# Six of eight query tiles projected in the slots of the stick-breaking attention

## The chip, the cores and the metric

The kernel runs on one core of one Trainium2 chip. The metric is device time in microseconds of one execution. Before the change three runs took 2627.49, 2628.47 and 2636.64 us; the median is 2628.47.

## The reference

Two blocks run one after the other on a sequence of 512 tokens with 1024 features. The first holds two layers of chunked attention with relative bias beside retention. The second holds four feed-forward layers (width 2816), a convolution layer and one layer of stick-breaking attention with 16 heads of 64 features. The change touches that attention and the projections at its two sides:

```python
q = split_heads(u @ attn_w_q[i])
# stick_breaking_attention, per block of 128 queries, keys up to the block's end
z = jnp.einsum('bhqd,bhkd->bhqk', qb, kb) * scale
causal = s_pos < t_pos
log_beta = jax.nn.log_sigmoid(z)
log_one_minus = jnp.where(causal, jax.nn.log_sigmoid(-z), 0.0)
log_remain = lax.cumsum(log_one_minus, axis=3, reverse=True) - log_one_minus
weights = jnp.where(causal, jnp.exp(log_beta + log_remain), 0.0)
outs.append(jnp.einsum('bhqk,bhkd->bhqd', weights, vb))
# then
h = h + o @ attn_w_o[i]
```

## The kernel before, in words

All five engines run programs written out by hand; the order of the work on each is the order of the code, and semaphores tie them together. Features lie on partitions, tokens along the free axis. SyncE issues the DMAs of the weights, ScalarE rounds (names ending in `_hi`), GpSimd or VectorE subtracts to get the low part (`_lo`), TensorE multiplies, VectorE empties PSUM.

**A product of full precision** is three matmuls: high by high, low by high, high by low (`product`, lines 1372 to 1374, moving 128x512). Weights come in chunks of 1 MB into `raw`, two slots in turn. The queries' weights `w_q` are four chunks of two output tiles (128 features, one pair of heads); a tile is 8 products. `w_o` is four chunks of the same form. In `layer("q")` all eight tiles are projected, chunk by chunk, into PSUM banks 0 to 3; VectorE scales each tile with the row's inverse root mean square into `sb_q` (line 924). Keys and values were spilled to DRAM before the third feed-forward layer and are read back while the first query chunk runs (lines 468 and 469).

**The stick-breaking attention** handles a pair of heads at a time and, within a pair, four key tiles of 128 keys, from the last to the first, against 128, 256, 384 and 512 queries. That gives 32 slots of two units (one a head). For unit u:

- TensorE, `sb_scores` (L1710 and the mask, L1714): three products of the split keys and queries, into one of six PSUM banks.
- VectorE, `sb_absolute` (L1320): the absolute value into `tmp`. ScalarE, `sb_decay` (L840, exponential) and `sb_logs` (L845, logarithm).
- VectorE, `sb_softplus` (L1326) and `sb_rounds` (L1336, `soft_hi`); GpSimd, `soft_low` (L567, `soft_lo`).
- TensorE, `sb_arguments` (L1724): cumulative sums by triangular matrices, added onto the scores in the same bank.
- ScalarE, `sb_weights` (L835): the exponential into `stick`.
- TensorE, `sb_sums` (L1735): values times weights, into bank 4 or 5 by the pair's parity. After a pair VectorE rounds and splits the output (L1355, L1356).

On TensorE slot i holds `sb_scores(i)`, `sb_arguments` of slot i-2 and `sb_sums` of slot i-3. `sb_scores(i)` waits until the weights of slot i-3 are made, since the banks are used again. VectorE's iteration i takes softplus and rounding of the first unit of slot i-1, the two absolute values of slot i, softplus and rounding of the second unit of slot i-1, and where i is 6, 10, 14 and so on the output of a pair. ScalarE's iteration i takes two decays of slot i, then weights (slot i-2) and logarithms (slot i) in turn. GpSimd also stages the split queries and keys of the next pair (`stage_sb`, L558 and L561) between its `soft_low` calls. `soft_hi` and `soft_lo` lie over `x_hi` and `x_lo`.

After slot 31 GpSimd makes the low parts of `w_o`, and `out_layer("o")` runs.

## Time and profile before

| | us |
|---|---|
| median of three runs | 2628.47 |
| profiled execution | 2627.77 |
| its span, first to last instruction | 2626.0 |
| TensorE busy in the span | 2528.4 (96%) |
| ScalarE / VectorE / GpSimd busy | 710.4 / 1060.3 / 1007.6 |
| mean granted TensorE clock | 0.984 of full |

A profile row has the start, the duration, the engine, the line of the kernel, the operation, and what it writes and reads. What stands in brackets is the idle time of that engine ahead of the row and the operation that ended it. PEld is TensorE's weight load, which runs beside matmuls. The queries' projection runs from 2012 to 2058 us, the attention from 2059.6 to 2200.3 us, the output projection from 2201.6 us on. A granted clock of 1.00 is 2.4 GHz, 0.50 is 1.2 GHz; a number between is a mean over a stretch.

### The profile page before, as it was taken

Reading aid. Unit: us, or ns where it says so; the run is one execution under the profiler, and the core shown is the slowest. Engines: PE = TensorE matmul, PEld = TensorE weight load, DVE = VectorE, ACT = ScalarE, POOL = GpSimd, SP = SyncE. Lnnn points to the kernel's source line nnn. Section 1 sums busy time; section 2 is a strip of 40 time slices with the busy share of each in tenths; the row PEclk is TensorE's granted clock in tenths of the full one; section 3 lists DMA queues with packets and bytes.
Section 4 is the critical chain, followed back from the end, with each engine's and each line's share of the span. In section 5 each row is a group of like instructions: output and inputs, shape, how many; then the busy total and the mean of one; then the engine's idle time right before and its main releaser. Section 6 shows DMA issues by size and latency. Waiting matters only on the chain.

```text
span 2626.0 us, 30302 instructions
## 1 busy us (share of the span) xinstructions
PE 2528.4 (96%) x11686; PEld 1999.7 (76%) x11686; DVE 1060.3 (40%) x1579; ACT 710.4 (27%) x912; POOL 1007.6 (38%) x327
## 2 busy tenths in 40 slices
...
DMA packets 42033, 235.83 MB, mean 90 GB/s; under 512 B 5344, under 2 KB 5344, under 8 KB 21472
## 3 DMA queue, kind: packets, MB, share of 16 engines
...
q8 instruction: 57, 0.93, 0.2%
...
## 4 chain that ended last, share of the span: by engine, by line
PE 89%; DVE 6%; issue 3%; ACT 2%; POOL 0%; SPq 0%; DMA 0%; DVEq 0%; ACTq 0%; POOLq 0%
PE ps L1372 27%; PE ps L1374 26%; PE ps L1373 26%; PE ps L1724 2%; PE ps L1646 1%; PE ps L1735 1%; PE ps L1608 1%; PE ps L1579 1%; PE ps L1615 1%; PE ps L1710 1%; PE ps L1558 1%; PE ps L1386 1%; PE ps L1567 1%; DVE small L1089 1%; DVE score L1083 0%
## 5 line engine op out<-in xcount | busy, mean ns | idle before, releaser
L489 POOL TENSOR_TENSOR w_lo<-raw,w_hi 128x2048 fp32r<-128x2048 f32 (+1 forms) x212 | 901.6, 4253 | 1430.5 <-ACT w_hi L598 1430.5
L1372 PE MATMUL ps<-x_hi,w_hi 128*128 128x512 f32 x2048 | 809.3, 395 | 20.6 <-DVE x_lo L875 18.1
L1374 PE MATMUL ps<-x_hi,w_lo 128*128 128x512 f32 x2048 | 800.1, 391 | 0.0
L1373 PE MATMUL ps<-x_lo,w_hi 128*128 128x512 f32 x2048 | 799.4, 390 | 0.0
L598 ACT ACTIVATE w_hi<-raw 128x2048 fp32r<-128x2048 f32 (+1 forms) x220 | 385.3, 1751 | 350.8 <-PE ps L1374 343.4
L1372 PEld LDWEIGHTS ps<-x_hi,w_hi 128*128 128x128 f32 x2048 | 385.8, 188 | 112.3 <-issue 29.3
L1374 PEld LDWEIGHTS ps<-x_hi,w_lo 128*128 128x128 f32 x2048 | 385.8, 188 | 81.5
L1373 PEld LDWEIGHTS ps<-x_lo,w_hi 128*128 128x128 f32 x2048 | 386.3, 189 | 77.4
L985 DVE TENSOR_TENSOR tmp<-ps,rms_b 128x512 f32<-128x512 f32 x88 | 60.9, 692 | 589.2 <-PE ps L1374 578.6
L1372 PE MATMUL ps<-hid_hi,w_hi 128*128 128x512 f32 x704 | 278.1, 395 | 0.0
L1374 PE MATMUL ps<-hid_hi,w_lo 128*128 128x512 f32 x704 | 278.1, 395 | 0.0
L1373 PE MATMUL ps<-hid_lo,w_hi 128*128 128x512 f32 x704 | 278.1, 395 | 0.0
L687 ACT ACTIVATE tmp<-tmp 128x512 f32<-128x512 f32 x88 | 55.8, 634 | 699.1 <-DVE tmp L985 699.0
L1010 DVE SCALAR_TENSOR_TENSOR x<-ps,x 128x512 f32 x32 | 22.1, 692 | 389.2 <-PE ps L1374 389.2
L1374 PEld LDWEIGHTS ps<-hid_hi,w_lo 128*128 128x128 f32 x704 | 132.0, 187 | 32.4
L1372 PEld LDWEIGHTS ps<-hid_hi,w_hi 128*128 128x128 f32 x704 | 132.0, 187 | 32.3
L1373 PEld LDWEIGHTS ps<-hid_lo,w_hi 128*128 128x128 f32 x704 | 132.0, 187 | 32.2
L660 ACT ACTIVATE tmp<-x 128x512 f32<-128x512 f32 (+1 forms) x64 | 39.8, 633 | 337.7 <-DVE x L1010 236.8
L883 DVE TENSOR_TENSOR sq_sum<-sq_sum,tmp 128x512 f32<-128x512 f32 x80 | 116.2, 1453 | 9.8 <-ACT tmp L660 7.3
L993 DVE TENSOR_TENSOR hid_lo<-tmp,hid_hi 128x512 f32 (+1 forms) x88 | 84.9, 964 | 10.6
L567 POOL TENSOR_TENSOR soft_lo<-tmp,soft_hi 128x128 fp32r<-128x128 f32 (+3 forms) x64 | 55.4, 866 | 69.5 <-DVE soft_hi L1336 69.5
L1372 PE MATMUL ps<-w_hi,x_hi 128*128 128x512 f32 x192 | 77.9, 406 | 2.8 <-issue 2.8
...
## 6 DMA issues: line engine op xcount, KB each, us to landing
...
```

The costliest lines, as they stand in the source:

```text
L489: nc.gpsimd.tensor_tensor(w_lo[:, s, 0:w], raw[:, s, 0:w], w_hi[:, s, 0:w].bitcast(f32), ALU.subtract).then_inc(lo_ready, 1)
L567: nc.gpsimd.tensor_tensor(soft_lo[:, soft_span(u)], tmp[:, u % 6, 0:SPAN[u % 8 // 2]], soft_hi[:, soft_span(u)].bitcast(f32), ALU.subtract ...
L598: nc.scalar.activation(w_hi[:, s, 0:w], raw[:, s, 0:w], ACT.Copy).then_inc(hi_ready, 1)
L660: nc.scalar.activation(tmp[:, slot, :], x[:, j, :], ACT.Square).then_inc(squares_ready, 1)
L687: nc.scalar.activation(tmp[:, s, :], tmp[:, s, :], func, bias=bias_col).then_inc(gate_out, 1)
L883: nc.vector.tensor_tensor(sq_sum[:, :], sq_sum[:, :], tmp[:, slot, :], ALU.add)\
L985: nc.vector.tensor_tensor(tmp[:, s, :], ps[:, 2 * s, :], rms_b[:, :], ALU.mult)\
L993: nc.vector.tensor_tensor(hid_lo[:, j, :], tmp[:, 2 + s, :], hid_hi[:, j, :].bitcast(f32), ALU.subtract).then_inc(hidden_ready, 1)
L1372: nc.tensor.matmul(out, hi, src_hi, start=start, stop=False, skip_group_check=True)
L1373: nc.tensor.matmul(out, hi, src_lo, start=False, stop=False, skip_group_check=True)
L1374: return nc.tensor.matmul(out, lo, src_hi, start=False, stop=stop, skip_group_check=True)
L1724: ins = nc.tensor.matmul(ps[:, Z_BANK[u % 6], P * (r - later):SPAN[r]], weights[:, :], part[:, at], start=False, stop=later == r and part ...
```

## The change

Only the first query chunk (tiles 0 and 1) and the first tile of the second stay ahead of the attention. The other 40 products are issued two a slot ahead of the scores in slots 0 to 19, all into bank 5. VectorE scales tile t = 3 to 7 in slot 4(t-3)+3 behind that slot's absolute values into one of three buffers, from which GpSimd stages pair t. `x_hi` and `x_lo` therefore stay alive, and `soft_hi`, `soft_lo` get regions of their own; `stick` has four buffers instead of six. Pairs 0 to 4 and 6 sum into bank 4, pairs 5 and 7 into bank 5. The low part of the third query chunk is made by VectorE in slot 1 in one operation of 128x2048. The fourth query chunk and the first two chunks of `w_o` are rounded by ScalarE and subtracted by VectorE in four pieces of 512 columns each, the slots given by two tables. `o_lo` lies by token tile over the values. GpSimd makes low parts of two query chunks and two output chunks only.

```diff
+Q_SLOTS = 5 * KD // 2
+PIECES = 4
+SB_HIGHS = {4: 0, 6: 1, 8: 2, 10: 3, 13: 4, 15: 5, 17: 6, 19: 7, 21: 8, 23: 9, 25: 10, 27: 11}
+SB_LOWS = {i + 1: n for i, n in SB_HIGHS.items()}
...
-    stick = region("stick", 16384, [P, 6, SEQ])
+    sb_q = region("sb_q", 12288, [P, 3, SEQ])
+    soft_hi = region("soft_hi", 13824, [P, 3328], f32r)
+    soft_lo = region("soft_lo", 17152, [P, 3328], f32r)
+    stick = region("stick", 20480, [P, 4, SEQ])
...
+    VALUE_BANK = [4, 4, 4, 4, 4, 5, 4, 5]
...
+    def sb_piece(n):
+
+        name, c = (("q", 3), ("o", 0), ("o", 1))[n // PIECES]
+        at = CHUNK // PIECES * (n % PIECES)
+        return first[name] + c, c % 2, slice(at, at + CHUNK // PIECES), n % PIECES == PIECES - 1
...
-        low_parts("q")
+        low_pair("q", 0)
...
+            if part == 0:
+                pool.wait_ge(sb_q_ready, pair + 1)
...
-        low_parts("o")
+        pool.wait_ge(lo_ready, first["o"] + 2)
+        low_parts("o", 1)
...
-        layer("q", nothing, norm=True)
+        high_part("q", 0, 1)
+        norm_root("q")
+        high_part("q", 1, 0)
...
-            if u >= 6:
-                act.wait_ge(sb_values, u - 5)
-            nc.scalar.activation(stick[:, u % 6, 0:n], ps[:, Z_BANK[u % 6], 0:n], ACT.Exp).then_inc(sb_exp, 1)
+            if u >= 4:
+                act.wait_ge(sb_values, u - 3)
+            nc.scalar.activation(stick[:, u % 4, 0:n], ps[:, Z_BANK[u % 6], 0:n], ACT.Exp).then_inc(sb_exp, 1)
...
+            if i in SB_HIGHS:
+                sb_high(SB_HIGHS[i])
...
-        pairs_of("q", scaled("q", sb_q, factor=SB_DIM ** -0.5))
...
+            if t < 2:
+                dve.wait_ge(chunk_done, first["q"] + 1)
+            elif t % 2:
+                dve.wait_ge(chunk_done, first["q"] + t // 2 + 1)
+            else:
+                dve.wait_ge(tile_done, 6 * DEPTH + t // 2)
+            if t >= 3:
+                dve.wait_ge(staged, 2 * (t - 2))
+            nc.vector.scalar_tensor_tensor(out=sb_q[:, t % 3, :], in0=ps[:, t if t < 2 else 5, :],
+                                           scalar=SB_DIM ** -0.5, in1=rms_b[:, :], op0=ALU.mult,
+                                           op1=ALU.mult).then_inc(sb_q_ready, 1)
...
+            if i % 4 == 3 and i < Q_SLOTS:
+                sb_query(3 + i // 4)
...
+            if i == 1:
+                dve.wait_ge(lo_ready, first["q"] + 2)
+                low("q", 2)
+            if i in SB_LOWS:
+                sb_low(SB_LOWS[i])
...
-        layer("q", "q", "q")
+        pe.wait_ge(banks_free[0], uses["q"])
+        pe.wait_ge(x_updated, updates["q"] + KD - 1)
+        two_tiles("q", 0, 0, x_split, KD * split_no["q"],
+                  {KD - 2: lambda: norm_sums("q"), KD - 1: lambda: norm_rows("q")})
+
+        def query_products(start, end):
+
+            for n in range(start, end):
+                c, t, k = 1 + n // (2 * KD), n // KD % 2, n % KD
+                s, at = c % 2, (KD * t + k) * P
+                if n % (2 * KD) == 0:
+                    pe.wait_ge(lo_ready, first["q"] + c + 1)
+                if k == 0 and n:
+                    pe.wait_ge(sb_q_ready, 2 + n // KD)
+                ins = product(ps[:, 5, :], w_hi[:, s, at:at + P], w_lo[:, s, at:at + P], x_hi[:, k, :],
+                              x_lo[:, k, :], k == 0, k == KD - 1)
+                if k == KD - 1:
+                    ins.then_inc(chunk_done if t else tile_done, 1)
+
+        query_products(0, KD)
...
+            if i < Q_SLOTS:
+                query_products(KD + 2 * i, KD + 2 * i + 2)
             if i < slots:
                 sb_scores(i)
```

TensorE at the start of the attention, before (L1372 to L1374 are a product, L1710 scores, L1714 masks):

```order
L1372 MATMUL ps<-x_hi,w_hi 128x512
L1373 MATMUL ps<-x_lo,w_hi 128x512
L1374 MATMUL ps<-x_hi,w_lo 128x512
L1710 MATMUL ps<-sb_qk_hi 128x128 x2
L1710 MATMUL ps<-sb_qk_lo,sb_qk_hi 128x128 x2
L1710 MATMUL ps<-sb_qk_hi,sb_qk_lo 128x128 x2
L1714 MATMUL ps<-mask_r,ident_r 128x128 x2
L1710 MATMUL ps<-sb_qk_hi 128x256 x2
L1710 MATMUL ps<-sb_qk_lo,sb_qk_hi 128x256 x2
L1710 MATMUL ps<-sb_qk_hi,sb_qk_lo 128x256 x2
```

TensorE at the same place now (L1436 to L1438 are a product, L1792 scores, L1796 masks), from the scores of slot 0 to the first of slot 1:

```order
L1792 MATMUL ps<-sb_qk_hi 128x128 x2
L1792 MATMUL ps<-sb_qk_lo,sb_qk_hi 128x128 x2
L1792 MATMUL ps<-sb_qk_hi,sb_qk_lo 128x128 x2
L1796 MATMUL ps<-mask_r,ident_r 128x128 x2
L1436 MATMUL ps<-x_hi,w_hi 128x512
L1437 MATMUL ps<-x_lo,w_hi 128x512
L1438 MATMUL ps<-x_hi,w_lo 128x512
L1436 MATMUL ps<-x_hi,w_hi 128x512
L1437 MATMUL ps<-x_lo,w_hi 128x512
L1438 MATMUL ps<-x_hi,w_lo 128x512
L1792 MATMUL ps<-sb_qk_hi 128x256 x2
```

Two products now stand between the scores of neighbouring slots.

VectorE in the first slots, before (L1320 absolute value, L1326 softplus, L1336 rounding):

```order
L1336 CAST soft_hi<-tmp 128x128
L1320 TENSOR_SCALAR tmp<-ps 128x256 x2
L1326 SCALAR_TENSOR_TENSOR tmp<-ps,tmp 128x128
L1336 CAST soft_hi<-tmp 128x128
L1326 SCALAR_TENSOR_TENSOR tmp<-ps,tmp 128x256
L1336 CAST soft_hi<-tmp 128x256
L1320 TENSOR_SCALAR tmp<-ps 128x384 x2
```

VectorE there now (L1375, L1381 and L1391 are the same three, L1265 the low part of the third chunk):

```order
L1391 CAST soft_hi<-tmp 128x128
L1375 TENSOR_SCALAR tmp<-ps 128x256 x2
L1381 SCALAR_TENSOR_TENSOR tmp<-ps,tmp 128x128
L1391 CAST soft_hi<-tmp 128x128
L1265 TENSOR_TENSOR w_lo<-raw,w_hi 128x2048
L1381 SCALAR_TENSOR_TENSOR tmp<-ps,tmp 128x256
L1391 CAST soft_hi<-tmp 128x256
L1375 TENSOR_SCALAR tmp<-ps 128x384 x2
```

The low part of 2048 columns stands ahead of the softplus of slot 1 and the absolute values of slot 2.

VectorE in slots 14 and 15 now (L1363 a piece's low part, L1417 and L1419 a pair's output, L1352 the scaling of a query tile):

```order
L1375 TENSOR_SCALAR tmp<-ps 128x384 x2
L1381 SCALAR_TENSOR_TENSOR tmp<-ps,tmp 128x256
L1391 CAST soft_hi<-tmp 128x256
L1363 TENSOR_TENSOR w_lo<-raw,w_hi 128x512
L1417 CAST o_hi<-ps 128x512
L1419 TENSOR_TENSOR o_lo<-ps,o_hi 128x4x128
L1422 MEMSET small 128x1
L1381 SCALAR_TENSOR_TENSOR tmp<-ps,tmp 128x384
L1391 CAST soft_hi<-tmp 128x384
L1375 TENSOR_SCALAR tmp<-ps 128x512 x2
L1352 SCALAR_TENSOR_TENSOR sb_q<-ps,rms_b 128x512
```

The piece stands between the rounding and the pair's output, and the scaling behind the absolute values of the slot.

## Rows read from the trace of the kernel before

**Rows 1.** Page, part 1: engines, busy us, share of the span, instructions.
```profile
PE 2528.4 (96%) x11686; PEld 1999.7 (76%) x11686; DVE 1060.3 (40%) x1579; ACT 710.4 (27%) x912; POOL 1007.6 (38%) x327
```

**Rows 2.** Busy time by stretches: length, engines (instructions), clock, DMA share, GB/s.
```profile
2060.00:2062.00 2.00, 2.00 (x18) 1.65 (x17) 0.54 (x3) 0.79 (x4) 0.00 (x0) 0.87 0.01 4
2078.00:2080.00 2.00, 2.00 (x15) 1.86 (x16) 0.94 (x3) 0.48 (x2) 0.00 (x0) 0.86 0.03 8
2109.30:2126.40 17.10, 14.23 (x90) 9.83 (x89) 11.63 (x28) 9.41 (x25) 10.55 (x13) 0.90 0.00 0
```

**Rows 3.** Timeline, TensorE in slots 10 to 12 and 28: start, duration.
```profile
2101.09 1.08 PE L1735 MATMUL ps<-stick,sb_v 128*64 128x512 f32 x4
2103.02 0.50 PE L1710 MATMUL ps<-sb_qk_hi 64*128 64x512 f32 x2 [0.85 <-ACT stick L835]
2107.72 0.33 PE L1710 MATMUL ps<-sb_qk_hi 64*128 64x128 f32 x2 [2.03 <-ACT stick L835]
...
2176.06 0.33 PE L1710 MATMUL ps<-sb_qk_hi 64*128 64x128 f32 x2 [2.02 <-ACT stick L835]
```

**Rows 4.** Timeline, VectorE and ScalarE, slots 10 to 13.
```profile
2102.24 0.69 DVE L1355 CAST o_hi<-ps 128x512 fp32r<-128x512 f32 x1
2104.57 1.28 DVE L1320 TENSOR_SCALAR tmp<-ps 128x512 int32<-128x512 int32 x2
2105.28 1.23 ACT L840 ACTIVATE tmp<-tmp 128x512 f32<-128x512 f32 x2 [1.91 <-DVE tmp L1320]
2107.20 0.38 ACT L835 ACTIVATE stick<-ps 128x256 f32<-128x256 f32 x1
2110.68 0.89 DVE L1336 CAST soft_hi<-tmp 128x128 fp32r<-128x128 f32 x1
```

**Rows 5.** Busy time by stretches, slots 11, 12 and 13.
```profile
2103.02:2107.72 4.70, 2.67 (x20) 1.92 (x21) 3.96 (x9) 2.79 (x7) 3.30 (x4) 1.00 0.00 0
2107.72:2112.07 4.35, 4.35 (x24) 3.08 (x24) 3.45 (x8) 2.26 (x7) 3.04 (x5) 0.68 0.02 4
2112.07:2116.64 4.57, 4.57 (x30) 3.40 (x28) 1.90 (x6) 2.33 (x6) 1.79 (x5) 0.93 0.00 0
```

**Rows 6.** Timeline, VectorE behind the second and third query chunk.
```profile
2036.30 1.29 DVE L924 SCALAR_TENSOR_TENSOR sb_q<-ps,rms_b 128x512 f32<-128x512 f32 x2 [7.64 <-PE ps L1374]
2047.18 1.29 DVE L924 SCALAR_TENSOR_TENSOR sb_q<-ps,rms_b 128x512 f32<-128x512 f32 x2 [9.59 <-PE ps L1374]
```

**Rows 7.** Refill's DMA issue, its time to landing, and GpSimd's staging.
```profile
2013.07 0.43 SPq L469 DMA_DIRECT2D sb_v<-v_spill  x1
...
sb_v<-v_spill SPq DMA_DIRECT2D x1, 2048.0 KB, 13.4
...
2042.90 0.61 POOL L558 CAST sb_qk_hi<-sb_q 128x512 fp32r<-128x512 f32 x1
...
2045.40 1.28 POOL L561 TENSOR_TENSOR sb_qk_lo<-sb_k,sb_qk_hi 128x512 fp32r<-128x512 f32 x1
```

**Rows 8.** Timeline, TensorE and ScalarE in slots 0 to 4.
```profile
2059.61 0.33 PE L1710 MATMUL ps<-sb_qk_hi 64*128 64x128 f32 x2 [1.58 <-DVE sb_q L924]
2065.21 0.99 ACT L840 ACTIVATE tmp<-tmp 128x384 f32<-128x384 f32 x2 [0.98 <-DVE tmp L1320]
2066.99 0.80 PE L1710 MATMUL ps<-sb_qk_hi 64*128 64x512 f32 x2 [2.09 <-ACT stick L835]
2072.24 0.47 PE L1710 MATMUL ps<-sb_qk_hi 64*128 64x128 f32 x2 [0.54 <-ACT stick L835]
```

**Rows 9.** Low parts: two by tile (ns min/median/max), then two of the timeline.
```profile
L1235 DVE TENSOR_TENSOR w_lo<-raw,w_hi x8: 2281/2287/3379, 1022.8 to 1107.5; 128x2048 fp32r<-128x2048 f32 x8
L993 DVE TENSOR_TENSOR hid_lo<-tmp,hid_hi x88: 691/693/3695, 662.4 to 2490.9; 128x512 f32 x86, 128x512 fp32r<-128x512 f32 x2
...
872.12 3.22 POOL L489 TENSOR_TENSOR w_lo<-raw,w_hi 128x1408 fp32r<-128x1408 f32 x1 [5.54 <-ACT w_hi L598]
872.21 3.68 DVE L993 TENSOR_TENSOR hid_lo<-tmp,hid_hi 128x512 f32 x1
```

**Rows 10.** Timeline, end of the attention.
```profile
2196.90 9.13 POOL L489 TENSOR_TENSOR w_lo<-raw,w_hi 128x2048 fp32r<-128x2048 f32 x2
2201.56 0.47 PE L1372 MATMUL ps<-o_hi,w_hi 128*128 128x512 f32 x1 [1.27 <-issue]
```

83 lines of the change are left out of this document (53 added, 30 removed).

## The prediction

> **What bounds the kernel now.** I read the page's table of engines first: TensorE is busy for 96% of the span [rows 1], so a gain must come where it is idle, waits or runs slowly. The busy time by stretches shows where: in the attention it is busy for 14.2 of every 17.1 us, and the granted clock is 0.90 there [rows 2]. Then I read the timeline of TensorE by slots. A slot i is scores(i), arguments(i-2), sums(i-3); four slots make a head pair, of 128, 256, 384 and 512 query columns (I call them r0 to r3), and from the scores of slot 12 (2107.72) to those of slot 28 (2176.06) four such periods take 68.3 us, 17.1 each [rows 3]. TensorE stands idle at two places of a period: 0.85 us before the scores of r3 and 2.03 us before those of r0, both times for the weights of three slots back (exponentials on ScalarE) [rows 3]. The wait before r0 ends a chain that starts on TensorE's last sum of r2 (begun 2101.09, 1.08 long, so 2102.2 [rows 3]): VectorE rounds the pair's output from 2102.24, then come softplus and, at 2104.57, two absolute values, on ScalarE two decays of 1.23 us in all, two weights and a logarithm between, until just before 2107.72 [rows 3, 4]. By slots: r3 with both idles 5.5 us, r0 4.35, r1 4.57, and 2.6 remain for r2. In r0 and r1 the clock is at 0.68 and 0.93 [rows 5]: for some 3.4 us (4.35 x 0.32 x 2 + 4.57 x 0.07 x 2) it stands at its lower level, 1.2 GHz, behind the idle of 2.03 us.
>
> **What is taken out ahead of the attention.** A query tile is 8 products of 3 matmuls. A chunk is two tiles, 48 matmuls, and lasts 2047.18 - 2036.30 = 10.88 us [rows 6], so a matmul is 0.227 us, a product 0.68. Of 64 products, 24 stay ahead and 40 move into slots 0 to 19, two a slot: 40 x 0.68 = 27.2 us leave the front, and 1.36 us enter each of 20 slots.
>
> When can the attention start? The first chunk ends near 2024.2, the eight products of tile 2 near 2030.7: before, the second chunk ends at 2036.3 [rows 6]; half a chunk is 5.4. The tile's scaling takes 0.69 us and the next product waits for it, since both use bank 5: 0.9 us idle. Two products follow, to 2033.0. Pair 0 must be staged by then: the second spill refill lands 13.4 us after 2013.07, at 2026.5 [rows 7], and staging takes 0.61 + 0.61 + 1.28 + 1.28, 3.8 us with its gaps [rows 7], so 2030.4. No stall. The scores of slot 0 start at 2033.0 instead of 2059.61 [rows 8], 26.6 us earlier.
>
> **Slots 0 to 3.** VectorE takes the third chunk's low part in slot 1, ahead of the softplus of slot 1: 2.29 us by the same operation elsewhere [rows 9]. Before, the first decay of slot 2 comes 5.60 us behind the scores of slot 0 and the scores of slot 3 come 1.78 behind that decay (2059.61, 2065.21, 2066.99 [rows 8]). The low part stands on VectorE between the two and pushes the decay by 2.29; the products ahead of slots 1 and 2 fall beside that. So the decay is at 2040.9 and scores(3) at 2042.7. That is 9.7 us behind scores(0) instead of 7.4. From there to scores(4) before: 5.25 us, all at the lower clock. Now the tile switch counts: product 16 waits for the scaling, which stands behind two absolute values of 512. Scores of 512 until VectorE reads them, 2.1 at the lower clock (1.3 at the full one: 2.6 - 1.36 below), absolute values 1.3, scaling 0.7, two products 1.4 at the full clock or 2.7 at the lower: 4.7 to 6.8, I take 6.0 since a stop of some us lies just ahead, as where the clock fell before. So scores(4) at 2048.7 against 2072.24: 23.5 us are left of the gain.
>
> **A period with query products, slots 4 to 19.** I take the end of the last sum of r2 as zero.
> - r3: products to 1.36, then scores, 0.5 later than before; the absolute values began at 2104.57, 2.4 [rows 4], when VectorE had had the scores for some 0.3 us, so they start at 2.6 and end at 3.9. The scaling 0.69 ends at 4.6; TensorE has been done with r3 since 1.36 + 2.67 (its busy time [rows 5]) = 4.03. Products of the next tile to 6.0; the weights are there at 5.8. So 6.0 instead of 5.5, and the idle is 0.6 instead of 2.9.
> - r0: with that idle gone I expect the clock at its full level: 4.35 x 0.68 is 3.0, I take 3.1.
> - r1: 1.36 + 4.35 = 5.7. r2: 1.36 + 2.6 = 4.0. No idle was there to take the products.
> Sum 18.8, 1.7 us longer than before. Against that the plain count: 5.44 us of products, less 2.3 of idle, less 1.45 of clock.
>
> **The pieces.** The high and low parts of three chunks go to ScalarE and VectorE in twelve pieces each; the low ones at 0.69 us (a subtraction of 128x512 with two sources [rows 9]), the high ones at 0.6, half of the two decays of 512 [rows 4]. Where they hang on no chain they cost nothing: VectorE is busy for 1.90 of r1's 4.57 us, ScalarE for 2.33 [rows 5]. They cost at three places. The four pieces of the last query chunk end in slot 11, behind scaling, softplus and rounding, at 6.3 us instead of 4.6, and slot 12 waits for them: 1.7, and 0.7 for clock. In slots 14, 18, 22 and 26 a low piece stands ahead of the pair's rounding, in slots 15, 19, 23 and 27 a high one ahead of the weights: each on the chain above. With products around, r0 then starts at 6.85, not 6.0 (slots 16 and 20); without products at 5.5 + 0.69 + 0.6 = 6.8, 1.3 more than before (slots 24, 28), and 0.5 for the clock behind an idle of over 3 us.
> Six periods: 18.8 + 0.5 (clock still recovering), 18.8 + 2.4, 19.7, 19.7, 18.9, 18.9 = 117.7 against 2176.06 - 2072.24 = 103.8 [rows 3, 8], of which the first took 18.4 at the lower clock. Loss 13.9.
> At the end TensorE waits 1.27 us until VectorE's outputs are split and GpSimd has the low part of the first output chunk, a 4.6 us operation begun at 2196.90 [rows 10]; it is ready long before now: gain 1.3.
>
> **Sum.** 26.6 - 3.1 (slots 0 to 3) - 13.9 + 1.3 = 10.9. The profiled execution is 2627.77 (span 2626.0), 0.7 under the median of the three runs, 2628.47. 2627.8 - 10.9 = 2616.9; I say 2617. The new regions of SBUF, the strided low part of the output, four stick buffers for six and three query buffers I cost at nothing: the weights of slot i, made in slot i+2, need the sums of slot i-2, and those stand in slot i+1. Without that cover a weight would wait for one group of sums, 1.08 us at most [rows 3]; I take 0.
>
> **Unknown sizes.** A piece's low part beside GpSimd: alone 0.69, or 3.68 when begun 0.09 us behind a GpSimd operation of 3.22 [rows 9]: it waits until that one ends. GpSimd's operations between the slots are up to 1.28 us [rows 7], so a piece costs 0.69 to 2.4. I take 0.69, since GpSimd is idle where the critical pieces stand (staging ends before, and its next work comes from that rounding); with the other end at four places, +7 us.
>
> **Rivals.**
> 1. The products vanish in the waits and the pieces in idle time: TensorE alone sets the period at 14.2 - 1.45 + 5.44 = 18.2, last periods 17.1. For it: TensorE's order is fixed and nearly full. Against it: the chain behind the pair's rounding. -23.5 + 4 x 1.1 - 1.3 - 1.3 (slot 4's first period was 18.4) = -21.7: 2606.
> 2. Pieces and GpSimd block each other: every critical piece waits for a whole operation, and roundings wait too (a cast of 128 columns takes 0.89 us at 2110.68 [rows 4], longer than a subtraction of 512). 2616.9 + 7 + about 2 = 2626: no change.
> The Trainium skill, SBUF — State Buffer, section "Who interferes with whom", states that a VectorE tensor_tensor with both inputs in SBUF excludes a GpSimd operation that reads SBUF, and that the order of issue decides who blocks. The 3.68 us row agrees. By the rule VectorE would win where its piece follows its own rounding directly, which gives my 2617; were GpSimd in flight at all of them, this rival's time.
> 3. Slower: the lower clock. It came in at 2062 behind an idle of 1.58 us and a sparse opening, and left near 2078 [rows 2, 8]. If the stops at 2031, 2042 and in every r3 keep it there through the 20 slots with products, r0 takes 5.9 us (4.35 x 0.68 / 0.5), the other slots grow alike and products double: some 32 us a period instead of 19. It decides from 0.9 of such a period on, 25 us of half clock; all five give +50: 2667, with two 2630. Against it: more work fills the gaps than before.
>
> **How the numbers follow.** Forecast 2617 with its own range 2611 to 2623: 0.50. Rival 1: 0.26. Rival 2: 0.17. Rival 3: 0.07. The range 2606 to 2627 takes in most of rivals 1 and 2 and leaves out rival 3 and the far ends. A change below 0.5%, 13 us, can't be told from none here: faster means below 2615.3. Rival 1 and a quarter of the forecast's own range give 0.39; slower needs most of rival 3, 0.04; the rest, 0.57, is within.
>
> **What would show it.** Scores of slot 0 near 2033; slot 4 near 2049; periods 18.8 to 19.7 with the scores of r0 behind a TensorE idle of about 0.6 us; one longer stop at slot 12; a granted clock near 1.0 from slot 4 to 19; periods 5 and 6 longer than 17.1 by 1 to 2 us. Wrong if periods with products stay near 17.1 or pass 21, if the clock stays at half, or if slot 0 waits for staging.

## The result, and the profile after

The changed kernel takes 2619.43 us (median of 8 runs, 2613.31 to 2621.20) against 2631.28 for the kernel before (8 runs, 2627.49 to 2636.64): ratio 0.9948, 95% interval 0.9934 to 0.9961. The forecast was 2617, range 2606 to 2627. The profiled execution is the fastest of the eight, 2613.31 us with a span of 2611.6. It began the attention's refill 1.97 us earlier than the profiled execution of before, ahead of every instruction that the change moves (the first issue is at 2010.73, before at 2012.70), and this is taken off below. It is variation between executions: in versions with the same code up to there, the scores of slot 0 start anywhere from 2028.82 (x10) to 2035.35 (x6).

The page of after, its engines: TensorE has the same work in a span 14.4 us shorter, and GpSimd 11.5 us less [rows 1].

```profile
PE 2520.8 (97%) x11686; PEld 1990.6 (76%) x11686; DVE 1070.0 (41%) x1592; ACT 710.5 (27%) x921; POOL 996.1 (38%) x323
```

The timeline of after, TensorE at the start of the attention, answering to [rows 8]: the switch to tile 3's bank, the first scores, the stop ahead of the first arguments, that ahead of scores(3), the next tile switch, scores(4).

```profile
2029.73 0.47 PE L1436 MATMUL ps<-x_hi,w_hi 128*128 128x512 f32 x1 [0.88 <-DVE sb_q L1352]
...
2031.26 0.33 PE L1792 MATMUL ps<-sb_qk_hi 64*128 64x128 f32 x2
...
2038.25 0.33 PE L1806 MATMUL ps<-soft_hi,neg_upto 128*128 128x128 f32 x1 [0.96 <-POOL soft_lo L586]
...
2040.83 0.50 PE L1792 MATMUL ps<-sb_qk_hi 64*128 64x512 f32 x2 [0.71 <-ACT stick L854]
...
2044.14 0.47 PE L1436 MATMUL ps<-x_hi,w_hi 128*128 128x512 f32 x1 [0.63 <-DVE sb_q L1352]
...
2045.70 0.33 PE L1792 MATMUL ps<-sb_qk_hi 64*128 64x128 f32 x2
```

Busy time of after by stretches: slots 0 to 3, then four of the six periods (slots 8 to 11, 16 to 19, 20 to 23, 24 to 27), then slot 28 up to the output projection (length, busy time of TensorE, its weight loads, VectorE, ScalarE, GpSimd, granted clock, DMA share, GB/s). [Rows 2, 5] had 14.23 busy of 17.10 at a clock of 0.90.

```profile
2031.26:2045.70 14.44, 12.14 (x73) 8.57 (x72) 10.98 (x24) 7.23 (x20) 7.23 (x7) 1.00 0.21 73
...
2065.22:2086.21 20.99, 19.00 (x114) 13.01 (x114) 14.53 (x32) 10.21 (x27) 12.47 (x14) 1.00 0.04 6
...
2106.09:2125.95 19.86, 17.39 (x107) 11.99 (x108) 13.44 (x31) 10.33 (x27) 11.38 (x13) 1.00 0.00 1
2125.95:2144.11 18.16, 14.17 (x89) 9.67 (x89) 12.81 (x30) 10.32 (x27) 11.41 (x13) 0.91 0.17 59
2144.11:2162.33 18.22, 14.23 (x88) 10.19 (x89) 12.51 (x30) 10.31 (x27) 11.29 (x12) 0.90 0.00 1
...
2162.33:2187.83 25.50, 23.07 (x128) 15.53 (x128) 14.18 (x32) 11.85 (x29) 9.85 (x10) 0.87 0.12 42
```

The next table puts every kernel on the same marks: s(i) is the start of the scores of slot i, o that of the output projection. In "clock" stand the granted clocks from s(20) to s(24), s(24) to s(28) and s(28) to o. Each ratio is to the kernel before on the same chip. x1 to x4 share one set of runs of before (median 2631.23), x5 to x8 another (2627.84), x9 to x11 a third (2633.96), x12 has 2633.99. The runs of before alone spread over 10 us (those above 2632 us have a mean clock of 0.981 to 0.983, those under 2629 one of 0.983 to 0.985), so medians are compared within a set, and ratios across sets.

| | s(0) to s(4) | periods from s(4) to s(28) | s(28) to o | s(0) to o | clock | median | ratio (95%) |
|---|---|---|---|---|---|---|---|
| before | 12.63 | 18.4, 17.1 x5 | 25.50 | 141.9 | .90 .90 .93 | 2631.28 | 1 |
| after | 14.44 | 19.5, 21.0, 19.9, 19.9, 18.2, 18.2 | 25.50 | 156.6 | .91 .90 .87 | 2619.43 | .9948 (.9934-.9961) |
| x1 o as before | 14.44 | 19.5, 22.2, 19.5, 19.2, 15.7, 20.2 | 25.98 | 156.7 | 1.00 .75 .87 | 2615.89 | .9943 (.9924-.9962) |
| x2 pieces moved | 14.42 | 19.5, 19.6, 19.5, 19.2, 17.1, 17.1 | 24.16 | 150.5 | .90 .90 .93 | 2608.54 | .9917 (.9897-.9938) |
| x3 no products | 14.13 | 18.5, 17.6, 18.3, 19.4, 21.3, 19.6 | 24.28 | 153.1 | .75 .84 .93 | 2609.71 | .9925 (.9898-.9951) |
| x4 third split | 13.35 | 19.5, 21.0, 19.9, 19.9, 19.7, 19.5 | 27.23 | 160.0 | .81 .84 .81 | 2618.56 | .9951 (.9930-.9972) |
| x5 moved and split | 13.36 | 19.5, 19.6, 19.5, 19.2, 18.6, 20.2 | 24.18 | 154.2 | .82 .75 .93 | 2611.03 | .9935 (.9918-.9951) |
| x6 scaling first | 14.00 | 19.4 x4, 17.1, 17.1 | 24.15 | 149.8 | .90 .90 .93 | 2608.32 | .9926 (.9909-.9942) |
| x7 spread | 13.34 | 17.8, 17.8, 16.9, 17.8, 18.9, 16.1 | 23.44 | 142.0 | 1.00 1.00 .93 | 2603.32 | .9910 (.9894-.9927) |
| x8 third on GpSimd | 13.28 | 19.5, 21.7, 22.2, 19.9, 18.2, 19.5 | 27.25 | 161.6 | .89 .84 .81 | 2617.77 | .9955 (.9936-.9974) |
| x9 before, filled | 14.87 | 17.8, 15.7 x5 | 24.03 | 135.0 | 1.00 1.00 .93 | 2619.28 | .9951 (.9935-.9966) |
| x10 spread, filled | 13.34 | 17.8, 17.8, 16.9, 17.8, 18.9, 16.1 | 23.95 | 142.5 | 1.00 1.00 .93 | 2601.02 | .9885 (.9866-.9904) |
| x11 after, filled | 14.42 | 19.5, 21.0, 19.9, 19.9, 16.8, 18.2 | 24.19 | 153.8 | 1.00 .91 .93 | 2613.05 | .9926 (.9906-.9946) |
| x12 after, filled more | 14.41 | 19.5, 22.3, 19.9, 20.9, 16.8, 16.8 | 22.72 | 153.2 | 1.00 1.00 1.00 | 2613.03 | .9925 (.9899-.9951) |

The account of after against before, between the two profiled executions ([rows 8] and the timeline above give the starts): s(0) is 28.35 us earlier, 26.4 without the 1.97; slots 0 to 3 cost 1.8; the six periods 116.6 - 103.8 = 12.8; from s(28) to o both need 25.50. That leaves 11.8. The medians differ by 11.85. That the two agree so closely is luck: after's profiled execution is 6.1 us under its own median, before's 3.5 us under its own.

### The profile page after: what moved, and what is told of

It reads as the page before. It is cut to its first block, busy times and chain, and to the rows that moved or that the text cites. A ratio compares the mean times of both kernels' runs of the same rounds, so it can differ in the third digit from the quotient of the medians.

```text
span 2611.6 us, 30315 instructions
## 1 busy us (share of the span) xinstructions
PE 2520.8 (97%) x11686; PEld 1990.6 (76%) x11686; DVE 1070.0 (41%) x1592; ACT 710.5 (27%) x921; POOL 996.1 (38%) x323
## 4 chain that ended last, share of the span: by engine, by line
PE 89%; DVE 6%; issue 3%; ACT 2%; POOL 0%; SPq 0%; DMA 0%; DVEq 0%; ACTq 0%; POOLq 0%
PE ps L1436 27%; PE ps L1438 26%; PE ps L1437 26%; PE ps L1806 1%; PE ps L1712 1%; PE ps L1674 1%; PE ps L1645 1%; PE ps L1681 1%; PE ps L1450 1%; PE ps L1624 1%; PE ps L1792 1%; PE ps L1633 1%; PE ps L1819 1%; DVE small L1119 1%; DVE score L1113 0%
## 5 line engine op out<-in xcount | busy, mean ns | idle before, releaser
L503 POOL TENSOR_TENSOR w_lo<-raw,w_hi 128x2048 fp32r<-128x2048 f32 (+1 forms) x208 | 883.2, 4246 | 1423.3 <-ACT w_hi L615 1423.3
L1436 PE MATMUL ps<-x_hi,w_hi 128*128 128x512 f32 x2048 | 811.2, 396 | 25.3 <-DVE x_lo L905 18.0
L1438 PE MATMUL ps<-x_hi,w_lo 128*128 128x512 f32 x2048 | 800.0, 391 | 0.0
L1436 PEld LDWEIGHTS ps<-x_hi,w_hi 128*128 128x128 f32 x2048 | 385.8, 188 | 124.6 <-issue 37.9
L615 ACT ACTIVATE w_hi<-raw 128x2048 fp32r<-128x2048 f32 (+1 forms) x217 | 379.7, 1750 | 336.8 <-PE ps L1438 329.0
L1438 PEld LDWEIGHTS ps<-x_hi,w_lo 128*128 128x128 f32 x2048 | 385.4, 188 | 81.4
L1436 PE MATMUL ps<-hid_hi,w_hi 128*128 128x512 f32 x704 | 278.1, 395 | 0.0
L1438 PE MATMUL ps<-hid_hi,w_lo 128*128 128x512 f32 x704 | 278.1, 395 | 0.0
L1436 PEld LDWEIGHTS ps<-hid_hi,w_hi 128*128 128x128 f32 x704 | 131.9, 187 | 32.4
L1438 PEld LDWEIGHTS ps<-hid_hi,w_lo 128*128 128x128 f32 x704 | 131.9, 187 | 32.4
L586 POOL TENSOR_TENSOR soft_lo<-tmp,soft_hi 128x128 fp32r<-128x128 f32 (+3 forms) x64 | 62.2, 972 | 68.4 <-DVE soft_hi L1391 68.4
L1436 PE MATMUL ps<-w_hi,x_hi 128*128 128x512 f32 x192 | 77.4, 403 | 2.8 <-issue 2.8
```

What stands on the lines that cost most here:

```text
L503: nc.gpsimd.tensor_tensor(w_lo[:, s, 0:w], raw[:, s, 0:w], w_hi[:, s, 0:w].bitcast(f32), ALU.subtract).then_inc(lo_ready, 1)
L586: nc.gpsimd.tensor_tensor(soft_lo[:, soft_span(u)], tmp[:, u % 6, 0:SPAN[u % 8 // 2]], soft_hi[:, soft_span(u)].bitcast(f32), ALU.subtract ...
L615: nc.scalar.activation(w_hi[:, s, 0:w], raw[:, s, 0:w], ACT.Copy).then_inc(hi_ready, 1)
L1436: nc.tensor.matmul(out, hi, src_hi, start=start, stop=False, skip_group_check=True)
L1438: return nc.tensor.matmul(out, lo, src_hi, start=False, stop=stop, skip_group_check=True)
```

## Experiments

**x1 and x2: what the pieces cost.** The first gives `w_o` back to GpSimd behind the attention (eight of twelve pieces less). The second only moves the pieces by a slot or so, away from the chain behind a pair's output and from slot 11.

```diff
# x1
-SB_HIGHS = {4: 0, 6: 1, 8: 2, 10: 3, 13: 4, 15: 5, 17: 6, 19: 7, 21: 8, 23: 9, 25: 10, 27: 11}
+SB_HIGHS = {4: 0, 6: 1, 8: 2, 10: 3}
...
-        low_parts("o", 1)
+        low_parts("o")
...
+            if i == slots + 1:
+                high_part("o", 0, 0)
...
# x2
+SB_HIGHS = {4: 0, 5: 1, 6: 2, 8: 3, 13: 4, 16: 5, 17: 6, 20: 7, 21: 8, 24: 9, 25: 10, 28: 11}
+SB_LOWS = {5: 0, 7: 1, 8: 2, 9: 3, 16: 4, 17: 5, 20: 6, 21: 7, 24: 8, 25: 9, 28: 10, 29: 11}
```

> The eight pieces for the output chunks are taken out of the slots; those two chunks are rounded and subtracted at the end, as in the kernel before. Theory (pieces ahead of a pair's output and ahead of the weights sit on the chain that releases the scores of r0): periods 5 and 6 (scores of slot 20 to 24, 24 to 28) fall from 18.16 and 18.22 us to 17.1 each, periods 3 and 4 from 19.88 and 19.86 to about 19.4 (TensorE's own work 18.75 and the tile switch 0.6); the stop of about 1.3 us ahead of the output projection returns. In sum 3.1 - 1.3 = 1.8 us shorter than the changed kernel. Rival (pieces run in idle time and the longer periods come from elsewhere, as more GpSimd contention or the strided output): all periods stay, and the kernel is 1.3 us longer than the changed one.

> All twelve pieces stay in the slots, but high pieces never in an r3 slot and low pieces never in an r2 slot, and the last piece of the fourth query chunk is low in slot 9 instead of 11. Theory: the stop ahead of slot 12's products (1.99 us) falls to the tile switch's 0.6, period 2 from 20.99 to 19.5; periods 3 and 4 to about 19.4, periods 5 and 6 to 17.1 to 17.3; no stop at the output projection. In sum about 1.4 + 0.9 + 2.0 = 4.3 us shorter than the changed kernel. Rival (a piece costs the same wherever it stands, since VectorE and ScalarE are the bound): periods unchanged within 0.3 us each.

x2 did what the step of the pieces says: the stop at slot 12 shrinks from 1.99 to 0.62 us and its period from 21.0 to 19.6, the last two periods return to 17.1, and the median is 10.9 under that of after, though across sets, by the ratios, it is 0.3%, 8 us. Timeline of TensorE in x2, slot 12:

```profile
2085.74 0.47 PE L1436 MATMUL ps<-x_hi,w_hi 128*128 128x512 f32 x1 [0.62 <-DVE sb_q L1352]
```

x1 removes the same critical pieces from slots 14 on and gains little. Its stretches show why (behind the stop of slot 12; slots 20 to 23; slots 24 to 27):

```profile
2085.00:2089.64 4.64, 2.85 (x6) 1.82 (x6) 2.81 (x6) 1.92 (x5) 2.65 (x2) 0.64 0.35 99
...
2128.33:2143.99 15.66, 12.78 (x89) 8.86 (x90) 12.12 (x28) 9.39 (x25) 11.14 (x13) 1.00 0.01 1
2143.99:2164.15 20.16, 17.29 (x88) 12.64 (x89) 10.95 (x28) 9.40 (x25) 10.50 (x13) 0.75 0.00 1
```

The last two rows are the same instructions. Behind an idle of 1.75 us the period took 15.66 us at the full clock; the next, behind 2.03 us, took 20.16, half of it at the lower clock; in before it is 17.1 at 0.90 behind 2.03 [rows 3]. So 17.1 is not a length of its own: it holds one fall of the clock to 1.2 GHz that costs 1.44 us. The length of the idle alone does not say whether the clock falls: ahead of slot 20 x2 has the same 1.75 us as x1 and takes 17.10 at 0.90. The theory had 34.2 us for the last two periods of x1; they take 35.8. And the wait for the output's low parts is back, 0.95 us ahead of o.

**x3: what the products cost.** Of each query tile in the slots only one matmul is left; the other products of the five tiles are left out, and the rest is as in after.

```diff
+                if n < KD:
+                    ins = product(ps[:, 5, :], w_hi[:, s, at:at + P], w_lo[:, s, at:at + P], x_hi[:, k, :],
+                                  x_lo[:, k, :], k == 0, k == KD - 1)
+                elif k == KD - 1:
+                    ins = nc.tensor.matmul(ps[:, 5, :], w_hi[:, s, at:at + P], x_hi[:, k, :], start=True,
+                                           stop=True)
```

> Leaves out the three matmuls of each of the 40 products in the slots but one matmul at the end of each tile, so the queries of pairs 3 to 7 are not what they should be; all waits, scalings and pieces stay. Theory: TensorE goes back to waiting on the chain, so its idle of 2.9 us a period and the lower clock (mean about 0.90) are back and periods 1 to 4 are 17.1 plus what the pieces cost, 17.3 to 18.3: only about 2 us a period shorter than with 5.4 us of products. Rival (the periods with products are long because of scalings and pieces on VectorE, not because of TensorE's work): the periods stay above 19.

The four periods from s(4) to s(20) hold 20.4 us of products (30 x 0.68: none stands ahead of slot 20), and without them the four are only 6.4 us shorter (80.25 against 73.85). TensorE's idle in them grows from 5.8 to 12.7 us, and the clock takes most of the rest, some 6 us by this sum. The first of the four by stretches:

```profile
2045.76:2064.23 18.47, 15.80 (x89) 11.10 (x90) 12.46 (x30) 10.44 (x27) 10.91 (x13) 0.84 0.00 1
```

The clock is 0.84 to 0.90 in the four, where after has 1.00. The periods of 18.5, 17.6, 18.3 and 19.4 us lie at the upper end of the expected 17.3 to 18.3 or above it, the last in the rival's range. The last two periods, in which nothing was edited, are 21.3 and 19.6 instead of 18.2, at 0.75 and 0.84.

**x4, x5, x8: the low part of the third chunk.** x4 cuts it into 512, 1024 and 512 columns in slots 0, 1 and 2; x5 is x2 with the same cut; x8 gives it whole to GpSimd behind the staging of pair 0.

```diff
# x4, x5
-            if i == 1:
-                dve.wait_ge(lo_ready, first["q"] + 2)
-                low("q", 2)
+            if i < 3:
+                sb_third(*((0, 1), (1, 3), (3, 4))[i])
...
# x8 (the same three lines of VectorE go)
+        pool.wait_ge(hi_ready, first["q"] + 3)
+        nc.gpsimd.tensor_tensor(w_lo[:, 0, :], raw[:, 0, :], w_hi[:, 0, :].bitcast(f32), ALU.subtract)\
+            .then_inc(lo_ready, 1)
```

> The low part of the third query chunk, one operation of 2.29 us on VectorE in slot 1, is made in three parts: 512 columns in slot 0, 1024 in slot 1, 512 in slot 2. Theory (that operation holds up slot 0's second unit on GpSimd and slot 2's absolute values on VectorE): the idles of 0.96 us ahead of the first arguments and 0.71 ahead of the scores of slot 3 shrink by 1 us together, scores(0) to scores(4) 14.44 goes to about 13.5. Rival (the opening is bound by the chain through ScalarE): 14.4 as before.

> The moved pieces of x2 together with the third chunk's low part in three parts over slots 0 to 2. Theory (the two costs lie in different slots and add up): scores(0) to scores(4) 13.4 us as in x4, periods as in x2 (19.5, 19.55, 19.5, 19.2, 17.1, 17.1), so about 1.1 us under x2's 2608.5. Rival (what the opening gains is given back at slot 4, since the tile switch there waits for the scaling anyway): slot 4's scores come as in x2 and the time is x2's.

> Undoes one part of the change alone: the third chunk's low part goes back to GpSimd, between the staging of pairs 0 and 1. Theory: 4.6 us there put the staging of pair 1 to about 2039 and with it slot 0's first soft part, 2.5 to 3 us later than in the changed kernel, while VectorE gains 2.29: scores(0) to scores(4) is 15.5 to 17 instead of 14.44. Rival (GpSimd has slack in the opening): 13.4 or less, as with the low part off VectorE's chain.

In slots 0 to 3 all three gain the same 1.1 us (14.44 to 13.35, 13.36, 13.28). In x8 I had it wrong: GpSimd has the time for 4.57 us there and holds up only one wait by 0.41.

```profile
2030.13 4.57 POOL L593 TENSOR_TENSOR w_lo<-raw,w_hi 128x2048 fp32r<-128x2048 f32 x1
...
2038.95 0.33 PE L1806 MATMUL ps<-soft_hi,neg_upto 128*128 128x128 f32 x1 [0.41 <-POOL soft_lo L586]
```

None of it reaches the time: x4 and x8 are at after's ratio, x5 is not under x2. The loss stands in stretches that the edit does not touch: x4's last two periods are 19.7 and 19.5 at 0.81 and 0.84 instead of 18.2 at 0.90, its end 27.23 instead of 25.50; x5's last two 18.6 and 20.2 at 0.82 and 0.75. That is one profiled execution of each; that the clock took the 1.1 us in the other runs too is inferred from the medians.

**x6: which wait ends last in r3.** On x2, the scaling stands ahead of the slot's absolute values instead of behind them.

> Undoes one part of the change on top of x2: a query tile is scaled ahead of the slot's two absolute values of 512, not behind them. Theory (in an r3 slot the absolute values are on the chain that releases the weights and so the scores of r0): TensorE's stop ahead of the next tile's first product (0.53 to 0.62 us) goes, but the scores of r0 now wait for the weights, since the absolute values start 0.2 to 0.7 later: the period changes by -0.1 to +0.4 us, in sum within 1.5 us of x2. Rival (the tile switch is the only bound in r3): each of the periods 19.5 falls by 0.5 to 0.6 us.

The stop of 0.62 at the tile switch goes and another comes, for the weights:

```profile
2068.71 0.33 PE L1792 MATMUL ps<-sb_qk_hi 64*128 64x128 f32 x2 [0.38 <-ACT stick L854]
```

A period goes from 19.5 to 19.4: two waits end at nearly the same time there, and 18.98 of 19.52 us were busy anyway. From s(0) to o it takes 149.8 us against 150.5 in x2, and the ratios of the two (0.9926 and 0.9917) can't be told apart.

**x7: fewer products a period.** The products of slots 0 to 19 go to slots 0 to 24, one where the slot has little idle, so that a period of four slots has four to seven instead of eight, and the last periods keep some; the pieces and the scalings move with them. Several edits at once: the third chunk's low part is split too, and the banks of the sums change.

```diff
-Q_SLOTS = 5 * KD // 2
+Q_AT = [2, 2, 2, 2, 2, 1, 1, 2, 2, 1, 1, 2, 2, 1, 0, 1, 2, 1, 1, 2, 2, 1, 1, 3, 3]
+Q_SCALES = {3: 3, 8: 4, 15: 5, 20: 6, 24: 7}
+SB_HIGHS = {4: 0, 5: 1, 8: 2, 9: 3, 16: 4, 17: 5, 20: 6, 21: 7, 25: 8, 28: 9, 29: 10, 32: 11}
+SB_LOWS = {5: 0, 8: 1, 9: 2, 12: 3, 17: 4, 20: 5, 21: 6, 24: 7, 28: 8, 29: 9, 32: 10, 33: 11}
...
```

> The 40 products are spread over slots 0 to 24 instead of 0 to 19, two or three in r3 and r0 slots and one in r1 and r2 slots; tiles are scaled in slots 3, 8, 15, 20 and 24, the pieces are moved accordingly, the third chunk's low part is split as in x4, and pair 6 instead of 5 and 7 sums in bank 5. Theory (with products TensorE is the bound: 13.3 us of its own work a period plus 0.68 a product, 19.5 with the tile switch; without them the period is the chain's 15.7 plus 1.4 for the lower clock): the 8 products taken from the first 20 slots shorten these by about 5 us, and the period from slot 20 to 24 grows by less, since they fill its idle of 2.6 us and keep the clock: scores(4) to scores(24) 94.85 in x2 falls to about 91, the total to 2604. Rival (the chain through VectorE and ScalarE bounds all periods alike): the sum of periods stays at 94.8.

```profile
2045.50:2063.26 17.76, 17.60 (x107) 11.92 (x107) 11.93 (x28) 9.74 (x26) 11.19 (x13) 1.00 0.00 1
...
2115.70:2134.60 18.90, 18.90 (x112) 13.02 (x112) 13.91 (x32) 10.50 (x27) 11.48 (x13) 1.00 0.00 1
2134.60:2150.69 16.09, 12.86 (x89) 8.85 (x89) 12.46 (x29) 9.32 (x25) 10.88 (x12) 1.00 0.19 66
```

TensorE is nearly full in the periods with products, and the clock is at 1.00 up to slot 28. From s(4) to s(24) it takes 89.1 us, where 91 was expected. From s(0) to o it takes 142.0 us, as long as before, with 25.8 us of products inside (38 x 0.68; two stand ahead of slot 0). The time is 2603.32 (2600.53 to 2603.72), by the ratios 0.4% under after. In its own set x6, which stands at x2's level, has 2608.32 (2605.93 to 2610.81): 5.0 us less, where the traces differ by 7.8 (149.8 to 142.0).

**x9 to x12: idle filled with matmuls that nobody reads.** From x1 on the suspect is the clock behind an idle. Here TensorE gets matmuls of 128x512 into a bank of their own ahead of the scores: six in r0 and three in r3, or eleven in r0 (x12). x9 does it to the kernel before from slot 4 on, x10 to x7 in slots 25 to 31, x11 and x12 to after in slots 20 to 31. All pairs sum into bank 4 in them.

```diff
# x11; in x12 11 stands for 6
+            if 20 <= i < slots:
+                for _ in range({0: 6, 3: 3}.get(i % 4, 0)):
+                    nc.tensor.matmul(ps[:, 5, :], neg_ones[:, :], x_hi[:, 0, :], start=True, stop=True,
+                                     skip_group_check=True)
```

> The kernel before, with idle time of TensorE filled by matmuls whose result nobody reads: from slot 4 on six of 128x512 into a bank of their own ahead of the scores of the slots with 128 columns (about 6 x 0.22 = 1.3 us in the 2.03 us idle) and three ahead of those with 512 columns (0.66 us in the 0.85 us idle); all pairs sum into one bank, so that bank 5 is free. Theory (a period of 17.1 us holds one fall of the clock behind the 2.03 us idle, and that costs 1.44 us): TensorE has 2 us more work in each period and still the periods shrink from 17.1 to about 15.7, granted clock 1.00 instead of 0.90, and the median falls by 6 to 10 us, to about 2622. Rival A (the period is the chain through VectorE and ScalarE, or the clock falls whatever stands in the gap): periods stay 17.1, median within 2 us of 2630. Rival B (the matmuls stand in the way of the scores): periods 17.4 or more, slower.

> The version with the products spread over 26 slots, with all pairs summed into one bank and the same matmuls without a reader in the slots without products (25 to 31). Theory: the last period goes from 16.1 to about 15.7, and the end of the attention, where the clock was 0.85 behind slot 28, stays at 1.00: 1 to 3 us less, about 2601. Rival: there the clock is at its full level already and the added matmuls only lengthen the slots: 2603 to 2605.

> The kernel after, with the same matmuls without a reader in slots 20 to 31 alone (all pairs sum into one bank). Theory (a good part of what the pieces cost in the last periods is the clock that falls behind idles of 2.5 and 3.1 us): periods 5 and 6 from 18.2 to 16.7 to 17, the end likewise, median 2619 to about 2613 and runs closer together. Rival (the pieces' time on the chain is all): periods stay at 18.2 or grow by what the matmuls take, 2619 or above.

> As the run before it (the kernel after, with matmuls without a reader in slots 20 to 31), but eleven instead of six ahead of the scores of 128 columns, so that of the 3.1 us idle there about 0.45 is left and not 1.5. Theory (what is left of an idle decides whether the clock falls): the sixth period goes from 18.2 to 16.8 like the fifth, both with the clock at 1.00; median 2611 to 2612. Rival (in that period the clock falls for another reason, or the longer row of matmuls delays the scores): the sixth period stays at 18.2, median 2613 or above.

x9, a period by stretches, and the timeline ahead of its r0, where the idle is 0.44 instead of 2.03:

```profile
2106.62:2122.28 15.66, 15.21 (x98) 10.40 (x99) 11.75 (x28) 9.42 (x25) 10.58 (x13) 1.00 0.00 1
```

```profile
2120.18 1.66 PE L1745 MATMUL ps<-w_hi,neg_ones 128*128 128x512 f32 x6
2122.28 0.33 PE L1712 MATMUL ps<-sb_qk_hi 64*128 64x128 f32 x2 [0.44 <-ACT stick L835]
```

Every period from slot 8 on is 15.7 instead of 17.1 with more work in it, and the kernel before gets as fast as the changed one: 2619.28, ratio 0.9951. The theory held with its number for the periods, and rivals A and B fell. For the time it was expected at 6 to 10 us: the profiled executions differ by 8.6 (2627.77 to 2619.16), the medians of the set by 14.7. The runs of before spread from 2627.39 to 2636.49 there, and the five runs of x9 lie within 3.3 us. That the spread of before is falls of the clock too is likely, but not shown: its profile is of one of the shorter runs. The stretch from s(0) to s(4) costs 2.2 us more than before (14.87 against 12.63), since slot 4's six matmuls stand in it, where the clock is at 0.50 already (2065.65 to 2073.14); 7.0 us are left from s(0) to o (141.9 - 135.0).

x11 and x12, slots 24 to 27 and the end:

```profile
2144.72:2162.89 18.17, 16.64 (x98) 11.22 (x98) 12.80 (x30) 10.33 (x27) 11.32 (x12) 0.91 0.00 1
2162.89:2187.08 24.19, 22.62 (x132) 15.14 (x132) 14.32 (x32) 11.84 (x29) 9.90 (x10) 0.93 0.13 45
```

```profile
2145.06:2161.82 16.76, 16.39 (x102) 11.32 (x103) 12.77 (x30) 10.31 (x27) 11.34 (x12) 1.00 0.00 1
2161.82:2184.54 22.72, 21.13 (x132) 13.85 (x132) 14.48 (x32) 11.83 (x29) 9.89 (x10) 1.00 0.14 48
```

With 1.5 us of the idle left the clock still fell in the last period (18.17), with 0.4 left it did not (16.76), and the end is 22.72 instead of 25.50. The median of x12 is nevertheless that of x11: its profiled execution lost elsewhere, 1.3 us behind the stop at slot 12 (22.3), which is not filled, and 1.05 us in slot 20, where the filler can start only once the query tile is scaled, 0.74 us into an idle of 2.5. x10 shows nothing of the kind: the last period stays at 16.1, where the clock was full already, the end is 0.5 longer with the clock at 0.93 as without filler, and s(0) to o goes from 142.0 to 142.5. The fall at its end comes later than I had thought, behind a wait for GpSimd of 0.98 us near 2163 that the filler does not touch. Its ratio is 0.9885 (0.9866 to 0.9904) against x7's 0.9910 (0.9894 to 0.9927), from different chips, and its profiled execution had s(0) 3.3 us earlier from upstream. So the theory has no support at that place, and whether x10 is faster than x7 stays open. Both beat the kernel before and after.

## Why the prediction was right, step by step

| step | forecast | profiled execution |
|---|---|---|
| start of the scores of slot 0, earlier by | 26.6 | 26.4 |
| slots 0 to 3, cost | 3.1 | 1.8 |
| six periods, cost | 13.9 | 12.8 |
| end, gain | 1.3 | 0 |
| sum | 10.9 | 11.8 |

1. **What is taken out ahead** held: the stop at the tile switch was to be 0.9 and is 0.88, no wait for staging. The forecast's end of the first chunk, 2024.2, does not lead to its end of tile 2, 2030.7 (half a chunk later is 2029.6), but the rest follows from 2030.7 alone, and with the 1.97 put back tile 2 ended at 2030.8.
2. **Slots 0 to 3.** The low part on VectorE delays scores(3), as said: it starts 9.57 us behind the scores of slot 0 (9.7 forecast). The mis-sized term is from there to scores(4), "I take 6.0": it is 4.87 since the clock stayed at 1.00. 4.7 was the lower end, worked out for the full clock. The stops of 0.96 and 0.71 did not bring it down. In before it fell in the opening, and x3, which has the stop of about 1 us ahead of slot 0 and a sparse opening without the products, shows it at 0.73 from s(0) to s(4). The low part's place is confirmed by x4 and x8, which get 1.1 us back by moving it. It holds up GpSimd as well, which the forecast left out: the operation of 128x128 that started 0.17 us behind it took 2.43 us, where the one before took 0.46, and it is the one that TensorE's stop of 0.96 waits for.

```profile
2035.60 2.29 DVE L1265 TENSOR_TENSOR w_lo<-raw,w_hi 128x2048 fp32r<-128x2048 f32 x1
2035.77 2.43 POOL L586 TENSOR_TENSOR soft_lo<-tmp,soft_hi 128x128 fp32r<-128x128 f32 x1 [1.50 <-DVE soft_hi L1391]
```

3. **Periods with products.** Forecast 19.3, 21.2, 19.7, 19.7; measured 19.5, 21.0, 19.9, 19.9. The tile switch idles 0.53 and 0.74 (0.6 said) and, at slot 12, 1.99 behind the last piece, as named:

```profile
2083.86 0.69 DVE L1363 TENSOR_TENSOR w_lo<-raw,w_hi 128x512 fp32r<-128x512 f32 x1
...
2084.61 0.50 PE L1436 MATMUL ps<-x_hi,w_hi 128*128 128x512 f32 x1 [1.99 <-DVE w_lo L1363]
```

   But the parts have errors that cancel. Slots 16 and 17 by stretches:

```profile
2106.09:2110.77 4.68, 4.68 (x30) 3.44 (x30) 4.07 (x9) 2.27 (x7) 3.48 (x4) 1.00 0.01 4
2110.77:2116.67 5.90, 5.90 (x35) 4.18 (x34) 1.90 (x6) 2.96 (x7) 3.28 (x6) 1.00 0.00 0
```

   Slots 20 and 21 without products, in x1 at the full clock and in x2 with a fall:

```profile
2128.33:2131.50 3.17, 3.17 (x25) 2.40 (x25) 3.07 (x8) 2.12 (x7) 2.44 (x3) 1.00 0.00 0
2131.50:2135.82 4.32, 4.32 (x29) 3.13 (x28) 2.78 (x7) 2.48 (x7) 3.02 (x6) 1.00 0.00 0
```

```profile
2125.95:2130.22 4.27, 4.27 (x25) 3.00 (x25) 4.17 (x9) 2.67 (x8) 3.55 (x3) 0.69 0.00 0
2130.22:2134.88 4.66, 4.66 (x30) 3.43 (x29) 2.65 (x8) 2.75 (x7) 2.50 (x6) 0.92 0.10 16
```

   r2 and r3 take 3.46 and 4.71 us in both. So the term "1.45 of clock" was right: 17.10 - 15.66 = 1.44, all of it in r0 and r1 (1.10 + 0.34), and r0 at the full clock is 3.17 where I took 3.1. What was sized too small is two products: they add 1.51 us to r0 and 1.58 to r1, not 1.36. A period with no piece on the chain is 19.5 (x2) where I had 18.8. On the other side terms were too large. The 0.5 for a clock still recovering in the first period did not come (clock 1.00). The stop at slot 12 costs 1.4 (20.99 against x2's 19.56), not 2.4. The pieces in slots 14, 15, 18 and 19 cost 0.4 and 0.7 (19.88 and 19.86 against 19.51 and 19.16), not 0.85 each; and the fourth period holds six products, not the eight that were counted, since none stands ahead of slot 20. That the four sums come within 0.2 us is therefore luck in part.
4. **The pieces.** In slots 18 and 19 they stand on the chain as drawn, 0.68 ahead of the rounding and 0.61 between the decays and the weights:

```profile
2119.36 0.68 DVE L1363 TENSOR_TENSOR w_lo<-raw,w_hi 128x512 fp32r<-128x512 f32 x1
2119.96 0.68 DVE L1417 CAST o_hi<-ps 128x512 fp32r<-128x512 f32 x1
```

```profile
2122.99 1.23 ACT L859 ACTIVATE tmp<-tmp 128x512 f32<-128x512 f32 x2 [2.49 <-DVE tmp L1375]
2124.13 0.61 ACT L872 ACTIVATE w_hi<-raw 128x512 fp32r<-128x512 f32 x1
2124.65 0.36 ACT L854 ACTIVATE stick<-ps 128x256 f32<-128x256 f32 x1
```

   They lengthen the idle ahead of r0 from 2.0 to 3.14 us, 1.1 of the 1.3 forecast. The added 0.5 for clock is the mis-sized part: in this execution the last two periods are 18.2, with a clock of 0.91 and 0.90, as low as before and no lower. In x4 it was 0.81 and 0.84, with 19.7 and 19.5: the forecast of 18.9 lies between.
5. **The end.** The wait of 1.27 us is gone, as forecast:

```profile
2186.77 1.13 PE L1819 MATMUL ps<-stick,sb_v 128*64 128x512 f32 x4
2187.83 0.50 PE L1436 MATMUL ps<-o_hi,w_hi 128*128 128x512 f32 x1
```

   But s(28) to o stays 25.50. TensorE was busy for 21.79 of it at a clock of 0.93 before and for 23.07 at 0.87 after: 1.28 us went to the clock, which stayed down for longer behind slot 28 (from there on, by stretches):

```profile
2162.33:2166.00 3.67, 3.67 (x18) 3.55 (x19) 2.87 (x7) 1.41 (x5) 1.95 (x2) 0.50 0.02 4
2166.00:2171.00 5.00, 5.00 (x29) 3.52 (x29) 1.99 (x6) 1.98 (x6) 1.89 (x3) 0.72 0.61 210
2171.00:2176.00 5.00, 4.24 (x25) 2.07 (x23) 2.98 (x7) 3.15 (x10) 1.27 (x2) 1.00 0.00 0
```

   By the middle row some 2.8 us of it are at 1.2 GHz (5.00 x 0.28 x 2), 6.5 in all, against 3.4 in a period of before. This step failed: I counted a wait that goes as time gained and did not ask what the clock does in the same stretch. Where the clock there was 0.93 as in before, the end took 24.2 to 24.3 us (x2, x3, x5, x11), so 1.3 was right for that clock. Why it stayed down longer in after is open: x3 has the same idle of 3.14 ahead of slot 28 and 0.93. x12, with that idle filled, has 22.72.
6. **Unknown sizes.** 0.69 for a piece was right. All twelve, by line (ns min/median/max):

```profile
L1363 DVE TENSOR_TENSOR w_lo<-raw,w_hi x12: 679/684/686, 2052.4 to 2165.2; 128x512 fp32r<-128x512 f32 x12
```

   None waited for GpSimd, so the end of 2.4 each, and rival 2 with it, did not come about. It was GpSimd that waited: behind each of the twelve it starts a `soft_low` 0.16 us after the piece has begun, and that one takes 0.38 us longer than the same operation elsewhere. The piece of slot 20, and GpSimd's operation of 512 columns without and with one:

```profile
2128.28 0.68 DVE L1363 TENSOR_TENSOR w_lo<-raw,w_hi 128x512 fp32r<-128x512 f32 x1
```

```profile
2126.79 1.28 POOL L586 TENSOR_TENSOR soft_lo<-tmp,soft_hi 128x512 fp32r<-128x512 f32 x1 [0.70 <-DVE soft_hi L1391]
2128.44 1.65 POOL L586 TENSOR_TENSOR soft_lo<-tmp,soft_hi 128x512 fp32r<-128x512 f32 x1 [0.36 <-DVE soft_hi L1391]
```

   With the Trainium skill's rule (SBUF — State Buffer, "Who interferes with whom"), that the order of issue decides who blocks, the trace agrees: VectorE's piece came first each time, as the forecast had said.

Rival 1 asked for 17.1 in the last periods and no cost of pieces; x2 has both, and by it the median falls to 2608.5, near its 2606. Its other number did not come: periods with products are 19.2 to 19.6 in x2, not 18.2. So of the distance between after and rival 1 the pieces' places are one part and the price of the products the other. Rival 3 did not come: no period with products in after is below 1.00. Its prices in the forecast don't agree with each other either: at 32 us a period instead of 19, two periods cost 26 and five 65, not 13 and 50. Its direction (the clock as the hidden term) was the right one to fear. The clock did fall in periods with products in other runs, behind the stop of 1.99 us at slot 12 (0.92 in x1 and x12, 0.96 and 0.88 in x8), but by far less than rival 3 supposed.

How much of the gain is the clock? In the forecast's count the 5.44 us of a period's products are paid in part by idle (2.3 us) and in part by the clock (1.45), and x3 bears that out: 6.9 us and some 6 us over four periods. x3 has 26 us less work on TensorE (115 matmuls) and by its ratio (0.9925, of two runs) is only some 6 us faster than after. x9 has none of the change and gets the same ratio by the clock alone. So what the products win in the clock, work without a reader wins too, and it does so in after as well where idle is left (x11: the period from s(20) goes from 18.2 to 16.8).
